# Attention inside an encoder block: value products as three split passes, probabilities scaled on GpSimd, scores and projections placed between value products

## What is computed

```python
# branch A (latent attention), 8 heads: queries and keys have a nope part (128) and a rope part (64)
s = (einsum('bhqd,bhkd->bhqk', qn_b, kn) + einsum('bhqr,bkr->bhqk', qr_b, kr)) * scale
p = softmax(s);  o = einsum('bhqk,bhkd->bhqd', p, v)
# branch B (grouped queries), 8 heads over 2 key/value heads, width 128
s = einsum('bngqd,bnkd->bngqk', q_b, k) * scale
p = softmax(s);  o = einsum('bngqk,bnkd->bngqd', p, v)
merged = sigmoid(gate_a) * (o_a @ w_br_a) + sigmoid(gate_b) * (o_b @ w_br_b)
```

## Time and profile before

| what | us |
|---|---|
| median of 3 runs (lowest to highest) | 2194.33 (2192.65 to 2194.97) |
| span of the profiled execution | 2192.3 |
| TensorE busy in it | 2110.8 (96%) |
| DVE busy | 875.9 (40%) |
| ACT busy | 564.0 (26%) |
| GpSimd busy | 4.7 (0%) |

### The profile page before, as it was taken

One profiled execution on the slowest core, in us unless ns is written; L12 is line 12 of the kernel. 1 busy time (PEld: TensorE's weight loads), 2 busy tenths in 40 slices (PEclk: granted clock), 3 DMA queues, 4 the chain that ended last, 5 costly groups with the idle time before them and its releaser, 6 DMA issues.

```text
span 2192.3 us, 26368 instructions
## 1 busy us (share of the span) xinstructions
PE 2110.8 (96%) x10319; PEld 1373.3 (63%) x10319; DVE 875.9 (40%) x1246; ACT 564.0 (26%) x998; POOL 4.7 (0%) x8
## 2 busy tenths in 40 slices
PE   7999999999999999999999899998999989998986
PEld 5787888888887777888888545353534444444432
DVE  4762667666676665346333301112020302021114
ACT  4263432222246664113222511010101110011102
POOL 0000000000000000000000000000000000000000
PEclk9999999999999999999999999999999999999999
DMA  9948675887760001533422799999999999999998
GB/s 364 385 162 297 231 259 200 318 305 280 281 231 25 25 1 57 178 131 128 164 87 87 309 392 408 426 426 428 427 427 427 428 428 427 427 428 427 426 422 308
DMA packets 144063, 634.81 MB, mean 290 GB/s; under 512 B 11986, under 2 KB 29544, under 8 KB 112756
## 3 DMA queue, kind: packets, MB, share of 16 engines
q1 hardware_dynamic: 139348, 625.38, 72.5%
q10 hardware_dynamic: 4640, 8.40, 1.0%
HBM read 621.15 MB, written 12.58 MB: 289 GB/s over the span
## 4 chain that ended last, share of the span: by engine, by line
PE 84%; DMA 12%; DVE 2%; ACT 1%; issue 0%; SPq 0%; DVEq 0%; ACTq 0%
PE bank L804 24%; PE bank L1311 23%; PE bank L806 13%; DMA e_wide<-in_w_e_up 10%; PE bank L1283 5%; PE bank L990 5%; PE bank L864 3%; PE bank L1083 3%; PE bank L1303 1%; PE bank L1071 1%; DMA e_slot<-in_w_e_down 1%; PE bank L1304 1%; PE bank L769 1%; PE bank L1293 1%; PE bank L1195 1%
## 5 line engine op out<-in xcount | busy, mean ns | idle before, releaser
L1311 PE MATMUL bank<-e_wide,xgT 128*64 128x512 f32 x1456 | 404.5, 606 | 42.7 <-DMA e_wide<-in_w_e_up 26.4
L1492 ACT ACTIVATE w_hi<-stage 128x1024 fp32r<-128x1024 f32 (+1 forms) x168 | 175.4, 1044 | 594.5 <-PE bank L804 339.8
L1918 DVE TENSOR_TENSOR w_lo<-stage,w_hi 128x1024 fp32r<-128x1024 f32 (+1 forms) x168 | 202.4, 1205 | 302.6 <-ACT w_hi L1492 302.0
L1311 PEld LDWEIGHTS bank<-e_wide,xgT 128*64 128x64 f32 x1456 | 130.8, 139 | 285.1 <-issue 284.2
L1311 PE MATMUL bank<-e_slot,xgT 128*64 128x512 f32 x584 | 207.0, 598 | 0.0
L1311 PE MATMUL bank<-e_wide,heT 128*64 128x512 f32 x672 | 167.4, 594 | 0.0
L804 PE MATMUL bank<-hT_hi,w_hi 128*128 128x512 f32 x512 | 159.1, 392 | 0.0
L804 PE MATMUL bank<-hT_lo,w_hi 128*128 128x512 f32 x512 | 157.9, 390 | 0.0
L804 PE MATMUL bank<-hT_hi,w_lo 128*128 128x512 f32 x512 | 157.7, 389 | 0.0
L2490 DVE TENSOR_TENSOR x<-x,bank 128x512 f32<-128x512 f32 x128 | 79.6, 682 | 191.8 <-PE bank L1304 190.3
L1993 DVE SCALAR_TENSOR_TENSOR ada_acc<-ada_tile,siluc,ada_acc 128x1024 f32<-128x1024 f32 x116 | 148.8, 1282 | 6.7 <-DMA ada_tile<-in_w_ada 1.0
(11 more groups left out here) (363 smaller groups left out, 2961.4 us busy)
## 6 DMA issues: line engine op xcount, KB each, us to landing
e_wide<-in_w_e_up SPq DMA_DIRECT2D x49, 2048.0 KB, 17.3
e_wide<-in_w_e_gate SPq DMA_DIRECT2D x42, 2048.0 KB, 15.1
e_wide<-in_w_e_down SPq DMA_DIRECT2D x42, 2048.0 KB, 17.2
ada_tile<-in_w_ada SPq DMA_DIRECT2D x156, 512.0 KB, 5.8
stage<-in_w_in SPq DMA_DIRECT2D x96, 512.0 KB, 6.6
e_slot<-in_w_e_gate SPq DMA_DIRECT2D x43, 1024.0 KB, 16.4
e_slot<-in_w_e_down SPq DMA_DIRECT2D x41, 1024.0 KB, 17.1
e_slot<-in_w_e_up SPq DMA_DIRECT2D x30, 1024.0 KB, 10.8
```

Source lines behind the costliest of these rows:

```text
L1311: last = mm(acc[h][64 * e:64 * e + 64, :], stationary(e), weights(h, e), start=first, stop=end)
L1492: A(w_hi[:, c % NSPLIT, :, 0:width], stage[:, c % NSTAGE, :, 0:width], ACT.Copy).then_inc(hi_ready, 1)
L1918: V.tensor_tensor(w_lo[:, c % NSPLIT, :, 0:width], stage[:, c % NSTAGE, :, 0:width], w_hi[:, c % NSPLIT, :, 0:width].bitcast(F32), ALU.sub ...
```

## The change

Values (`v_hi`, `v_lo`, `vg_hi`, `vg_lo`) and transposed probabilities (`pT_hi`, `pT_lo`) are kept as two fp32r tiles, so that a value product is three fp32r passes. ACT rounds the transposed bank (`probs_hi`), DVE takes the rest (`probs_lo`). The scaling by the inverse sums moves to GpSimd, and the sums are inverted in two halves. On TensorE, blocks 0 and 1 of the next g head's scores stand between the g head's value products, and the next step's first projection (rope part before an even step, nope queries before an odd one) ahead of the m head's last value product. The new tiles use four slots of the weight ring, so branch chunks 4 to 7 are loaded after the last value product. Hunks that only declare semaphores or move the first `normalise` are left out.

```diff
         krT_hi, krT_lo = at("C", 28 * KB, "krT_hi", [P, S], F32R), at("A", 68 * KB, "krT_lo", [P, S], F32R)
-        v_sb = at("A", 74 * KB, "v_sb", [P, T, 2, DH])
-        pT = at("A", 70 * KB, "pT", [P, 2, S])
+        v_hi, v_lo = at("A", 74 * KB, "v_hi", [P, T, 2, DH], F32R), at("ring", 28 * KB, "v_lo", [P, T, 2, DH], F32R)
+        vg_hi, vg_lo = at("ring", 16 * KB, "vg_hi", [P, T, KVG * DH], F32R), at("ring", 20 * KB, "vg_lo", [P, T, KVG * DH], F32R)
+        pT_hi, pT_lo = at("A", 70 * KB, "pT_hi", [P, 2, S], F32R), at("ring", 24 * KB, "pT_lo", [P, 2, S], F32R)
         qg_hi, qg_lo = at("A", 14 * KB, "qg_hi", [P, S], F32R), at("A", 46 * KB, "qg_lo", [P, S], F32R)
...
                     load_gate(7, c8 + AHEAD)
-                else:
+                elif c8 + AHEAD < 12:
                     load_branches(c8 + AHEAD - 8, c8 + AHEAD - 7)
                 load_ada_at(11, c8)
-            load_branches(AHEAD, 8)
...
                 sp.wait_ge(sig_out[i], 16 * 9)
+            sp.wait_ge(pv_done, 4 * (HM + HG))
+            load_branches(4, 8)
             sp.wait_ge(o_lo, HM + HG)
...
-            def project(i):
+            def queries(i):
+
+                pe.wait_ge(hw_lo, split_of(i, "uq"))
+                split_product(query_bank(i), by_k(4, lambda k: three(uq_hi[:, k, :], uq_lo[:, k, :], cqT_hi[:, k, :], cqT_lo[:, k, :])),
+                              True, True).then_inc(proj_done, 1)
+
+            def project_first(i):
                 pe.wait_ge(pro_ready, QUERY[i] + 1)
                 if i % 2 == 0:
                     pe.wait_ge(hw_lo, split_of(i, "uqr"))
                     split_product(bank[5][:, :], by_k(4, lambda k: three(uqr_hi[:, k, :, :], uqr_lo[:, k, :, :], cqT_hi[:, k, :], cqT_lo[:, k, :])),
                                   True, True).then_inc(proj_done, 1)
+                else:
+                    queries(i)
+
+            def project(i):
+
+                if i % 2 == 0:
                     if i:
                         pe.wait_ge(o_lo, 2 * i)
-                pe.wait_ge(hw_lo, split_of(i, "uq"))
-                split_product(query_bank(i), by_k(4, lambda k: three(uq_hi[:, k, :], uq_lo[:, k, :], cqT_hi[:, k, :], cqT_lo[:, k, :])),
-                              True, True).then_inc(proj_done, 1)
+                    queries(i)
                 pe.wait_ge(hw_lo, split_of(i, "uk"))
                 if i:
...
                 elif kt == 0 and a % 4 == 0:
-                    pe.wait_ge(proj_hi, rests(a // 2) + 5)
+                    pe.wait_ge(values_rest, 2 * (a // 4) + 2)
                 elif kt == 1:
                     pe.wait_ge(proj_lo, rests(a // 2 + 1))
                 if kt == 0:
                 last.then_inc(pT_done, 1)
             def times_v(a, kt):
-                pe.wait_ge(pT_ready, 4 * a + kt + 1)
+                pe.wait_ge(pT_rounded, 4 * a + kt + 1)
                 if kt == 0:
+                    if a == 0:
+                        pe.wait_ge(values_rest, 1)
+                    elif a % 4 == 1:
+                        pe.wait_ge(values_rest, 2 * (a // 4) + 3)
                     if a % 4:
                         pe.wait_ge(o_lo, a)
                     else:
                         pe.wait_ge(proj_lo, rests(a // 2) + 5)
-                v = v_sb[:, kt, a // 2 % 2, :] if a % 2 else zg[:, kt, (HG + KVG + a // 8) * DH:(HG + KVG + a // 8 + 1) * DH]
-                mm(bank[4][:, :], v, pT[:, kt % 2, :], start=kt == 0, stop=kt == 3).then_inc(pv_done, 1)
+                if a % 2:
+                    hi, rest = v_hi[:, kt, a // 2 % 2, :], v_lo[:, kt, a // 2 % 2, :]
+                else:
+                    cols = slice(a // 8 * DH, (a // 8 + 1) * DH)
+                    hi, rest = vg_hi[:, kt, cols], vg_lo[:, kt, cols]
+                mm(bank[4][:, :], hi, pT_hi[:, kt % 2, :], start=kt == 0, stop=False)
+                mm(bank[4][:, :], rest, pT_hi[:, kt % 2, :], start=False, stop=False)
+                pe.wait_ge(pT_ready, 4 * a + kt + 1)
+                mm(bank[4][:, :], hi, pT_lo[:, kt % 2, :], start=False, stop=kt == 3).then_inc(pv_done, 1)
             def attend_rest(a):
                 times_v(a, 0)
                 probs_t(a, 2)
                 times_v(a, 1)
                 probs_t(a, 3)
+                if a % 2 == 0 and a < 2 * HM - 2:
+                    gqa_scores(a // 2 + 1, (0,))
                 times_v(a, 2)
+                if a < 2 * HM - 2:
+                    if a % 2:
+                        project_first(a // 2 + 1)
+                    else:
+                        gqa_scores(a // 2 + 1, (1,))
                 times_v(a, 3)
             gqa_scores(0, range(4))
+            project_first(0)
             for i in range(HM):
                 project(i)
                 if i % 2 == 0:
...
                     if i % 2 == 0:
-                        pe.wait_ge(proj_hi, rests(i) + 6)
+                        pe.wait_ge(values_rest, i + 3)
                     elif i == 3:
                         pe.wait_ge(pro_ready, KEYS1 + 1)
                     transpose_item(QUERY[i + 1], 5, head_columns(i + 1))
                 attend_rest(2 * i)
                 if i < HM - 1:
-                    gqa_scores(i + 1, (0, 1))
+                    gqa_scores(i + 1, (2,))
                     probs_t(2 * i + 1, 0)
                     probs_t(2 * i + 1, 1)
-                    gqa_scores(i + 1, (2, 3))
...
-            def normalise(a):
-                b = a % 2
-                act.wait_ge(rinv_seq, a + 1)
-                for qb in range(4):
-                    last = A(probs[b][:, qb, :], probs[b][:, qb, :], ACT.Copy, scale=rsum[:, b, 4 + qb:5 + qb])
-                last.then_inc(p_ready, 1)
+            def probs_hi(a, kt):
+
+                act.wait_ge(pT_done, 4 * a + kt + 1)
+                if 4 * a + kt >= 2:
+                    act.wait_ge(pv_done, 4 * a + kt - 1)
+                A(pT_hi[:, kt % 2, :], bank[6 + kt % 2][:, :], ACT.Copy).then_inc(pT_rounded, 1)
...
                     head_ukv_hi(i + 1)
                     if i % 2:
                         head_uqr_hi(i + 1)
-                else:
+                probs_hi(2 * i, 0)
+                probs_hi(2 * i, 1)
+                if i == HM - 1:
                     act.wait_ge(s_done, 4 * (2 * i + 1) + 1)
                     hi(N_BR, 0)
                 if i == 0:
                     for b in range(4):
                         act.wait_ge(sig_out[b], 16 * 9)
-                exponentials(2 * i + 1, 12, range(3))
+                exponentials(2 * i + 1, 12, (0, 1))
                 if i < HM - 1:
                     item_hi(QUERY[i + 1])
                 else:
                     hi(N_BR + 1, 1)
+                exponentials(2 * i + 1, 12, (2,))
+                probs_hi(2 * i, 2)
                 exponentials(2 * i + 1, 12, (3,))
-                normalise(2 * i + 1)
+                probs_hi(2 * i, 3)
                 output_hi(2 * i)
                 if i < HM - 1:
-                    exponentials(2 * i + 2, i + 1, range(4))
-                    normalise(2 * i + 2)
-            hi(N_BR + 2, 2)
+                    exponentials(2 * i + 2, i + 1, (0,))
+                probs_hi(2 * i + 1, 0)
+                probs_hi(2 * i + 1, 1)
+                if i < HM - 1:
+                    exponentials(2 * i + 2, i + 1, (1,))
+                else:
+                    hi(N_BR + 2, 2)
+                probs_hi(2 * i + 1, 2)
+                if i < HM - 1:
+                    exponentials(2 * i + 2, i + 1, (2,))
+                probs_hi(2 * i + 1, 3)
+                if i < HM - 1:
+                    exponentials(2 * i + 2, i + 1, (3,))
             output_hi(2 * HM - 1)
...
-            def inverse_sums(a):
+            def inverse_sums(a, half):
                 b = a % 2
-                dve.wait_ge(exp_done, 4 * a + 4)
-                V.reciprocal(rsum[:, b, 4:8], rsum[:, b, 0:4]).then_inc(rinv_seq, 1)
-
-            def probs_transposed(a, kt):
-
-                dve.wait_ge(pT_done, 4 * a + kt + 1)
-                if 4 * a + kt >= 2:
-                    dve.wait_ge(pv_done, 4 * a + kt - 1)
-                V.tensor_copy(pT[:, kt % 2, :], bank[6 + kt % 2][:, :]).then_inc(pT_ready, 1)
+                dve.wait_ge(exp_done, 4 * a + 2 * half + 2)
+                V.reciprocal(rsum[:, b, 4 + 2 * half:6 + 2 * half], rsum[:, b, 2 * half:2 * half + 2]).then_inc(rinv_seq, 1)
+
+            def probs_lo(a, kt):
+
+                dve.wait_ge(pT_rounded, 4 * a + kt + 1)
+                V.tensor_tensor(pT_lo[:, kt % 2, :], bank[6 + kt % 2][:, :], pT_hi[:, kt % 2, :].bitcast(F32), ALU.subtract).then_inc(pT_ready, 1)
+
+            def values_lo(i):
+
+                for half in range(2):
+                    dve.wait_ge(proj_hi, rests(i) + 5 + half)
+                    part = slice(2 * half, 2 * half + 2)
+                    V.tensor_tensor(v_lo[:, part, :, :], bank[6 - half][:, :].rearrange("p (t e d) -> p t e d", t=2, e=2),
```

(41 more changed lines are left out.)

10 lines of the change are left out of this document (6 added, 4 removed).

## The result

The changed kernel takes 2218.5 us (median of four runs, 2214.9 to 2223.0) beside 2194.65 us of the kernel before on the same chip: a ratio of 1.0112, with an interval of 1.0097 to 1.0127. The forecast was 2196.3 with a range up to 2203.5, so the time lies well above both. The profiled execution took 2221.04 us, its span is 2219.2 us, 26.9 more than before.

A forecast was written before the change was run, and what follows sets the result against it. TensorE's queue was taken to bound the kernel, DVE and ACT having little to spare. Even steps -6.4, odd +5.0, start +1.4, end +1.45, hold-up +0.5 made +2.0 us on the profiled span: forecast 2196.3, range 2186.5 to 2203.5.

The forecast's parts named there:

- part 5: Normalising on GpSimd: a block bounded by 0.64 and 1.12 us, taken as 0.9, costing nothing; at 1.12, 3.2 us in all.
- Three passes: Value products on TensorE: twelve passes take 2.73 us in place of 3.63, 0.90 less per head, 14.4 over 16 heads.
- ACT and DVE in turn: Transposed probabilities, rounded by ACT then subtracted by DVE: load does not grow, order matters; even step 22.6 us, 1.7 less.
- Odd steps, the rounding behind L1631's wait: Steps 1, 3, 5: ACT's roundings queue behind rope weights awaiting nope scores; TensorE waits 1.8 us, the later head another 0.4.
- rival A: ACT and DVE keep up, without the waits in even and odd steps: 7.8 us less, 2186.5; chance 0.25.
- Projection ahead of the last value product: Before even steps, nope queries wait bare for the output's rest, 1.6 us; in step 3 a key transposition waits about 0.7 longer.
- rival B: GpSimd paces the step, normalised halves coming later than the transposes, from 1.0 us a block: 2203; chance 0.30.
- The hold-up of DVE by GpSimd: DVE subtractions with two SBUF inputs might wait for a running GpSimd instruction: 0 to 4.5 us, taken as 0.5.
- Start: Before the first rope: two more DVE operations of 1024 columns make TensorE's value projection wait 1.4 us.
- End: Step 7 and after: chunk 0 0.7 later, last head's products save 0.25, gates 1.0 late (0 to 2.5); +1.45 us.
- rival C: Gates and chunks land late at the end, 2.5 us instead of 1.0: 2198; with the forecast, chance 0.45.

## Why the prediction was wrong

The step that failed is part 5. Everything else in the sum comes to within 5 us.

1. **Three passes.** Right in mechanism and size: with the wait for GpSimd gone and the interleaving in, the even step is 22.75 (forecast 22.6).
2. **ACT and DVE in turn.** Right. The 0.15 us that an even step is above my figure is a little more waiting for rests (the third pass waited up to 0.3).
3. **Odd steps, the rounding behind L1631's wait.** Right, to some tenths. In the changed kernel's step 1, which starts at 680.74, ACT first and then DVE:

```profile
682.56 0.63 ACT L1663 ACTIVATE uqr_hi<-wq 128x512 fp32r<-128x512 f32 x1 [2.40 <-PE bank L993]
683.10 1.07 ACT L1723 ACTIVATE pT_hi<-bank 128x512 fp32r<-128x512 f32 x2
```

```profile
683.71 1.29 DVE L2284 TENSOR_TENSOR pT_lo<-bank,pT_hi 128x512 fp32r<-128x512 f32 x2 [2.54 <-ACT pT_hi L1723]
684.92 0.68 DVE L2267 TENSOR_REDUCE nmax<-bank 128x1 f32<-128x512 f32 x1
...
688.38 0.67 DVE L2206 TENSOR_TENSOR qg_lo<-bank,qg_hi 128x512 fp32r<-128x512 f32 x1
```

   The maxima start at +4.2 (forecast 4.2), the query rests end at +8.3 (forecast 8.3). TensorE's wait is 2.05 us (forecast 1.8). With it rival A, in which ACT and DVE keep up, is out.
4. **Projection ahead of the last value product.** Right: 1.57 us bare (forecast 1.6), and 0.81 in step 3 (about 0.7). Together the odd step is 31.8 to 32.0, 0.3 to 0.5 above the 31.5 forecast.
5. **GpSimd.** Wrong. The term "one block: 0.64 to 1.12" was mis-sized: 1.55 us and more. The point from which rival B decides, 1.0 us a block, held (at 1.0 the even step is 22.76), so the rival's mechanism was the real one, with a price that I cut off at a bound that did not bind. I took a multiplication of two tensors as an upper bound for one of a tensor and a scalar, and nothing in the trace said so. At 1.55 us, four blocks from the inverted sums at 5.96 on end at 12.2, against transposes at 10.1: 2.1 late, and 2.0 to 2.2 were measured. Seven steps make 14 us. A bound left open upwards would have made room for these 14 us. Part 5's own sum was slightly high besides: by its times four blocks at 1.12 end 0.34 us late in an even step, not 0.5. And of the four blocks behind the 1.12 (4.48 us together) three took 1.04 us and one 1.49, so the trace of before already had this instruction at some 1.0 a block.
   What no term had was the clock: behind six of the seven waits TensorE ran most of the next 4.5 us at 1.2 GHz, 1.4 us each time. That is 8.4 in the profile of the changed kernel; net of the falls behind other waits it is some 3 of the median (18.3 us for all of GpSimd's work, less 14 for the waits and 1.1 at the start, leaves 3.2).
   The hold-up of DVE by GpSimd, 0 to 4.5 us in my sum, was next to nil here: it went the other way. Where DVE subtracted two operands from SBUF beside it (L2309 and L2213 at the start, L2218 in the odd steps, L1962 at the end), DVE kept its time, but for 0.1 us once (L2213 at 679.45, 0.79), and GpSimd stretched, from 6.2 us for four blocks to 6.75, 6.33 and 7.69. Alone, at 643.43, the subtraction of 1024 columns takes 1.23; the others stand beside GpSimd:

```profile
643.43 1.23 DVE L2324 TENSOR_TENSOR vg_lo<-zg,vg_hi 128x1024 fp32r<-128x1024 f32 x1
...
647.58 0.67 DVE L2309 TENSOR_TENSOR qr_lo<-q_rot,qr_hi 128x512 fp32r<-128x512 f32 x1
...
691.23 0.68 DVE L2218 TENSOR_TENSOR uqr_lo<-wq,uqr_hi 128x512 fp32r<-128x512 f32 x1
...
874.17 1.22 DVE L1962 TENSOR_TENSOR w_lo<-stage,w_hi 128x1024 fp32r<-128x1024 f32 x1
```

```profile
647.71 6.75 POOL L2639 TENSOR_SCALAR probs_g<-probs_g,rsum 128x512 f32<-128x512 f32 x4 [647.27 <-DVE rsum L2279]
...
688.56 6.33 POOL L2639 TENSOR_SCALAR probs_m<-probs_m,rsum 128x512 f32<-128x512 f32 x4 [7.98 <-DVE rsum L2279]
...
871.04 7.69 POOL L2639 TENSOR_SCALAR probs_m<-probs_m,rsum 128x512 f32<-128x512 f32 x4 [6.33 <-DVE rsum L2279]
```

   The Trainium skill, "SBUF — State Buffer", section "Who interferes with whom", says that whoever issues first gets the shared ports for the whole instruction and that the other blocks fully. At 691.23 and at 874.17 DVE issued second, and by the page it should have waited; it did not. Of GpSimd's 64 blocks 57 took 1.56 or 1.57 us, and all 7 longer ones stood beside such a DVE instruction; no run isolated it. Beside GpSimd's other instruction L2218 took 0.90 instead of 0.68 us, so DVE is not always spared.
6. **Start.** +2.45 instead of +1.4. The two operations were 0.69 and 1.23 us, as thought, and the value projection waits 1.08 for the rope's rest (1.4 forecast). Most of the other 1.4 is part 5 again: the start has its own wait for GpSimd, the 1.1 of the waits' last row.
7. **End.** +2.7 instead of +1.45. The gates came later than my 1.0, closer to rival C's 2.5: SP's issue, the first gate product on DVE and the fifth chunk in the changed kernel are

```profile
893.12 1.42 SPq L644 DMA_DIRECT2D sg_in<-sig_gates  x2
...
903.38 0.69 DVE L2405 TENSOR_TENSOR mT<-bank,sg_in 128x512 f32<-128x512 f32 x1 [9.51 <-DMA sg_in<-sig_gates]
...
904.22 0.70 PE L807 MATMUL bank<-oT_hi,w_hi 128*128 128x512 f32 x2 [1.71 <-DVE mT L2405]
```

   From issue to gate product are 10.3 us, where the earlier trace rows have 5.7. With the gates asked for first, the wait is gone and 2.4 us with it.

The account of what I expected without GpSimd (2195.8) and what the kernel without scaling took (2200.2): 1.2 us at the end, 3 x 0.3 in the odd steps, 4 x 0.15 in the even ones, and one or two falls of the clock behind the 2.05 us waits of the odd steps (its profile has one, 1.4 us). These falls also explain why moving L1663 brought 7.0 us instead of 3 x 1.7 = 5.1. That part is an inference from the profiles; only behind the wait for GpSimd was the idle time filled as a test.

My figure for the interleaving was wrong too, though only in an expectation: on top of three passes it is worth 2.4 us net. I had counted the wait for each head's last rest in full.

## What to carry to other kernels

An instruction that the trace does not show has no upper bound in another form of instruction on the same engine, even one that reads more; leave the range open on that side, or measure the block alone first. When work goes to an idle engine, compare its time with the slack between the moment its input is there and the moment its result is wanted (here 4.1 us for four blocks): a per cent of busy time says nothing of it. And a wait of some two microseconds on TensorE can cost more than its length, 1.4 us more in these steps. These runs give no length that is safe everywhere; filling a wait helped, but net by less than the falls it took away.
